# The four norm borders of a fused transformer kernel, row tile by row tile

## The chip, the cores and the metric

The kernel runs on one core of one Trainium2 chip. The metric is the device time of one execution in microseconds (us), lower is better. Each engine of the core (TensorE, VectorE, ScalarE, GpSimd, and SyncE, which only starts transfers here) runs its own list of instructions in the order in which the program wrote it, and waits for semaphores of the others. Nothing in such a list overtakes what stands ahead of it.

## The reference

The input x is 512 rows of 1024 numbers in float32. Three blocks and a feed-forward part follow each other, all of one form: normalise, project, mix, project back, normalise, add.

```python
def rms_norm(x, gain):
    y = xf * lax.rsqrt(jnp.mean(xf * xf, axis=-1, keepdims=True) + NORM_EPS)
    return y * gain
# hybrid_layer, twice (three kinds of attention between the projections)
h = rms_norm(x, g_pre);  p = h @ w_in
...
return x + rms_norm(y, g_post)
# second_block: a recurrence beside an attention, then a feed-forward part
h = rms_norm_2(x, pre_mix_norm[l]);  proj = h @ w_in[l]
...
x = x + rms_norm_2(mix, post_mix_norm[l])
h = rms_norm_2(x, pre_ffn_norm[l])
f = (jax.nn.silu(h @ w_ffn_gate[l]) * (h @ w_ffn_up[l])) @ w_ffn_down[l]
x = x + rms_norm_2(f, post_ffn_norm[l])
```

So there are four places at which x is normalised with a gain `g_pre` and then multiplied by weights: ahead of layer 0, of layer 1, of the third block and of the feed-forward part. They are called borders 0 to 3 here. At borders 1 to 3, and at the end of the kernel, the output y of the part before is first normalised with a gain `g_post` and added to x.

## The kernel before

**Tiles.** The 512 rows are four row tiles of 128. `x_res` holds x as [128, tile, 1024]. A product needs the normalised x the other way round, features on the partitions: `act_hl` holds it as eight chunks of 128 features by 512 rows. Every operand is split into a high part in a narrower format and a low part (what the high part leaves out), and each product of two numbers is three matmuls, high by high, high by low, low by high (`three`; lines 578 to 580 where the output's partitions are features, "feat", and 581 to 583 where they are rows, "tok").

**Weights.** They come as 274 blocks of 512 KB in a ring of four slots. SyncE loads a block into `w_raw` when the block four before it has been used; ScalarE makes its high part (`high`, line 792), GpSimd its low part (`low`, line 561), both into `w_hl`; then TensorE uses it in 24 matmuls of 512 columns. One dense group is four such blocks (BC = 2 chunks each) into banks 0 to 3.

**A border.** ScalarE and VectorE run `post(i)`: per row tile VectorE drains the last half of y from its bank (lines 1197, 1201), ScalarE squares it and makes the row's factor (`row_scale`, lines 799 to 803, 512 wide for y, since the other half was squared earlier in `first_half`, line 1018), VectorE multiplies y by the factor and by `g_post` (line 1467) and adds it to x (line 1469). ScalarE then squares x (line 799, 1024 wide) and VectorE multiplies the identity by the row's factor (line 1123, `diag`, which lies in `y_tok`). TensorE multiplies x by that diagonal: this transposes and scales at once (line 631, float32, which the chip does in two passes, 32 of them in a border, in two halves of four chunks). ScalarE takes the high part out of the bank with the gain as its scale (line 829), VectorE the low part (line 1135). The first four chunks are turned before the first weight block is used, the other four behind it. The first product needs all four row tiles.

**What sets the order.** `plan()` writes one list, STEPS, and each engine walks it, taking from each step what is its own. The last output projection before a border goes tile by tile (`tile_by_tile`), so that row tile 0 is done early. `high(b + 2)` is called at the first use of block b. At borders 1 and 2 ScalarE starts two more transfers on its own queue: `x_spill` (line 1075, x to memory, 2 MB) right behind the first high parts of the norm, and at border 2 with it `w_gates` (line 1077, 1 MB, the weights of the recurrence's gates), which TensorE wants at line 737.

**The end.** `post(3)` drains a tile of `y_ffn` one tile ahead of the arithmetic on it; each finished tile is stored by SyncE.

## Time and profile before

| | |
|---|---|
| median of 3 runs | 2050.96 us (2048.58 to 2052.0) |
| the profiled execution | 2051.6 us, of which its span 2049.8 us |
| TensorE matmul busy | 1941.4 us, 95% of the span, mean granted clock 0.966 |
| VectorE, ScalarE, GpSimd busy | 773.1, 886.3, 661.9 us |
| chain that ended last | TensorE 83%, VectorE 8%, ScalarE 5%, issue 3% |
| DMA | 163.80 MB, mean 80 GB/s |

Times in the profile count from the span's start. A row of the timeline gives the start and the duration of an instruction (or of several merged ones: x8), its engine, its line, what it writes and reads, and in brackets how long the engine sat idle before it and who ended that. The duration includes a fixed part that overlaps the next instruction: the distance between two starts is what an engine loses. In the stretches view, "PEclk" is the TensorE clock that was granted, as a share of full speed (1.0 is 2.4 GHz, 0.5 is 1.2 GHz). "128*128" in a matmul's row is the loaded operand.

### The profile page before, as it was taken

What the parts mean: (1) busy time and instruction counts of PE and PEld (TensorE: products, weight loads), DVE (VectorE), ACT (ScalarE), POOL (GpSimd) and SP (SyncE); (2) the same over time, 40 slices, a digit from 0 to 9 for tenths busy, and PEclk for the clock granted to TensorE, in tenths of its full rate; (3) what the DMA queues carried; (4) which work ended last, traced back from release to release, by engine and by line L of the source; (5) the groups of instructions that cost most, each with busy time, mean ns of one, the idle gap of its engine ahead of it and who ended that gap; (6) DMA issues with size and microseconds to landing.
All of it is one profiled execution on the core that took longest, in us unless ns stands there. A gap on an engine that the chain in (4) does not pass through costs nothing.

```text
span 2049.8 us, 25677 instructions
## 1 busy us (share of the span) xinstructions
PE 1941.4 (95%) x9552; PEld 1599.9 (78%) x9552; DVE 773.1 (38%) x1393; ACT 886.3 (43%) x1741; POOL 661.9 (32%) x278
## 2 busy tenths in 40 slices
PE   8998998998899899899889999999999989999998
PEld 6877787877777778787767788888788878888886
DVE  3434655344543555534444682111251431111102
ACT  4555564344455555444444652333453353322222
POOL 2422231321224132132123354434303424344442
PEclk9999999997899999999889999999999989999999
DMA  4221211211322112121032223222201322323222
GB/s 149 83 72 42 72 62 51 74 62 43 133 75 80 52 62 64 50 83 60 34 136 92 81 94 102 83 93 92 82 1 58 128 83 93 103 93 99 97 93 92
DMA packets 44572, 163.80 MB, mean 80 GB/s; under 512 B 6192, under 2 KB 6448, under 8 KB 43824
## 3 DMA queue, kind: packets, MB, share of 16 engines
q1 hardware_dynamic: 42640, 148.65, 21.9%
q10 hardware_dynamic: 1824, 13.63, 1.8%
q8 instruction: 77, 1.26, 0.2%
q14 instruction: 31, 0.25, 0.0%
HBM read 155.97 MB, written 6.29 MB: 79 GB/s over the span
## 4 chain that ended last, share of the span: by engine, by line
PE 83%; DVE 8%; ACT 5%; issue 3%; DMA 0%; POOL 0%; DVEq 0%; ACTq 0%; POOLq 0%; SPq 0%
PE bank L578 12%; PE bank L579 12%; PE bank L580 12%; PE bank L581 10%; PE bank L583 10%; PE bank L582 10%; PE bank L691 3%; PE bank L709 2%; PE bank L669 2%; PE bank L715 2%; PE bank L670 1%; ACT q_dup L904 1%; PE bank L711 1%; PE bank L667 1%; PE bank L631 1%
## 5 line engine op out<-in xcount | busy, mean ns | idle before, releaser
L561 POOL TENSOR_TENSOR w_hl<-w_raw,w_hl 128x1024 fp32r<-128x1024 f32 x274 | 661.7, 2420 | 1363.5 <-ACT w_hl L792 1362.8
L792 ACT ACTIVATE w_hl<-w_raw 128x1024 fp32r<-128x1024 f32 x274 | 287.4, 1058 | 344.8 <-DMA w_raw<-wstream 344.2
L578 PE MATMUL bank<-act_hl,w_hl 128*128 128x512 f32 x1056 | 428.2, 405 | 3.2 <-DVE act_hl L1135 2.5
L580 PE MATMUL bank<-act_hl,w_hl 128*128 128x512 f32 x1056 | 414.6, 393 | 0.0
L579 PE MATMUL bank<-act_hl,w_hl 128*128 128x512 f32 x1056 | 414.1, 392 | 0.0
L581 PE MATMUL bank<-w_hl,act_hl 128*128 128x512 f32 x672 | 265.7, 395 | 4.0 <-POOL w_hl L561 1.9
L583 PE MATMUL bank<-w_hl,act_hl 128*128 128x512 f32 x672 | 262.9, 391 | 0.0
L582 PE MATMUL bank<-w_hl,act_hl 128*128 128x512 f32 x672 | 262.7, 391 | 0.0
L578 PEld LDWEIGHTS bank<-act_hl,w_hl 128*128 128x128 f32 x1056 | 200.7, 190 | 45.6 <-DVE act_hl L1135 2.9
L580 PEld LDWEIGHTS bank<-act_hl,w_hl 128*128 128x128 f32 x1056 | 199.8, 189 | 43.7
L579 PEld LDWEIGHTS bank<-act_hl,w_hl 128*128 128x128 f32 x1056 | 200.6, 190 | 40.0 <-issue 1.9
L955 ACT ACTIVATE pt_hl<-bank 128x512 fp32r<-128x512 f32 (+3 forms) x128 | 56.0, 438 | 236.1 <-PE bank L691 235.7
L581 PEld LDWEIGHTS bank<-w_hl,act_hl 128*128 128x128 f32 x672 | 126.9, 189 | 31.8 <-issue 2.1
L583 PEld LDWEIGHTS bank<-w_hl,act_hl 128*128 128x128 f32 x672 | 126.9, 189 | 26.8
L582 PEld LDWEIGHTS bank<-w_hl,act_hl 128*128 128x128 f32 x672 | 127.1, 189 | 25.6
L1323 DVE TENSOR_TENSOR pt_hl<-bank,pt_hl 128x512 fp32r<-128x512 f32 (+3 forms) x128 | 62.5, 489 | 145.2 <-ACT pt_hl L955 144.5
L691 PE MATMUL bank<-ident,probs 128*128 128x128 f32 x508 | 94.4, 290 | 14.0 <-DVE pt_hl L1323 13.7
L1287 DVE TENSOR_REDUCE nmax<-bank 128x1 f32<-128x512 f32 (+3 forms) x128 | 60.2, 488 | 107.2 <-PE bank L678 105.9
L669 PE MATMUL bank<-k_hl,q_dup 128*128 128x512 f32 (+1 forms) x192 | 70.8, 369 | 16.6 <-DVE probs L1312 14.6
L1217 DVE TENSOR_TENSOR probs<-bank,probs 128x512 f32<-128x512 f32 x22 | 15.1, 688 | 186.4 <-PE bank L580 186.4
L581 PE MATMUL bank<-w_hl,y_hl 128*128 128x512 f32 x192 | 79.9, 416 | 5.2 <-DVE q_low L1231 5.2
L709 PE MATMUL bank<-vhl,pt_hl 128*128 128x128 f32 x320 | 84.6, 325 | 0.0
(216 smaller groups left out, 2907.9 us busy)
## 6 DMA issues: line engine op xcount, KB each, us to landing
w_raw<-wstream SPq DMA_DIRECT2D x274, 512.0 KB, 3.4
x_spill<-x_res ACTq DMA_DIRECT2D x2, 2048.0 KB, 6.9
x_res<-x_spill ACTq DMA_DIRECT2D x2, 2048.0 KB, 7.9
x_res<-x SPq DMA_DIRECT2D x4, 512.0 KB, 6.3
g_post<-post_gains ACTq DMA_DIRECT2D x4, 512.0 KB, 3.8
x_res<-x ACTq DMA_DIRECT2D x1, 2048.0 KB, 7.8
out<-x_res SPq DMA_DIRECT2D x4, 512.0 KB, 2.6
probs<-w_gates ACTq DMA_DIRECT2D x1, 1024.0 KB, 9.7
```

Source lines behind the costliest of these rows:

```text
L561: nc.gpsimd.tensor_tensor(w_hl[:, slot, 1].rearrange("p c n -> p (c n)"), w_raw[:, slot, :], w_hl[:, slot, 0].rearrange("p c n -> p (c n)" ...
L578: pe.matmul(out_ap, wh, ah, start=start, stop=False)
L579: pe.matmul(out_ap, wh, al, start=False, stop=False)
L580: return pe.matmul(out_ap, wl, ah, start=False, stop=stop)
L581: pe.matmul(out_ap, ah, wh, start=start, stop=False)
L582: pe.matmul(out_ap, ah, wl, start=False, stop=False)
L583: return pe.matmul(out_ap, al, wh, start=False, stop=stop)
L669: pe.matmul(to[:, 0:nb * P], q_dup[:, p, a, rows], k_hl[:, p, a, keys], start=True, stop=False)
L691: tr = pe.transpose(to[:, kb * P:(kb + 1) * P], probs[:, p_slot(kind, n, a), kb * P:(kb + 1) * P], ident[:, :])
L709: pe.matmul(o, pt_hl[:, slot, 0, keys], v.rearrange("p h d -> p (h d)"), start=(kb == 0), stop=False)
L792: nc.scalar.activation(w_hl[:, b % RING, 0].rearrange("p c n -> p (c n)"), w_raw[:, b % RING, :], ACT.Copy).then_inc(s_high_done, 1)
L1323: nc.vector.tensor_tensor(pt_hl[:, m % 3, 1, 0:nb * P], ps, pt_hl[:, m % 3, 0, 0:nb * P].bitcast(f32), ALU.subtract).then_inc(done, 1)
```

## The change

The four borders go row tile by row tile. `border(i, ...)` writes for each row tile t: drain and scale (`rows`), the turn of the tile (`normturn`), the sum of the next tile (`total`), and then those products of the first dense group whose rows are split. In "tok" groups (borders 0 and 1) that is a product per tile; in "feat" groups (borders 2 and 3) one per pair of tiles, in 256 columns. Blocks 0 and 1 of the group need chunks 0 to 3 of the norm, blocks 2 and 3 chunks 4 to 7.

The row factor and `g_pre` are now applied to rows, by one VectorE operation of 1024 columns into `y_acc` (`norm_row`), for which `g_pre` is a row repeated on 128 partitions (512 KB, as `g_post` was). TensorE transposes plainly, with the identity, eight transposes a tile into two banks. ScalarE's high part and VectorE's low part are two operations of 512 columns a tile. The sum y times factor times `g_post` plus x is three half-width operations instead of two full-width ones, and the first half of y has been multiplied by `g_post` ahead of the border (`half_gain`). The spill and the load of `w_gates` come behind the whole first group. The high parts of the group's blocks 4 and 5 are made when blocks 2 and 3 end. At the end of the kernel VectorE drains a tile and sums it, one after the other.

```diff
+    def border(i, dense_steps):
+        blocks, rest = dense_steps[:4], dense_steps[4:]
+        def part(ks, j):
+            if groups[blocks[0][2]]["orient"] == "tok":
+                return [blocks[k][:4] + ((j,),) for k in ks]
+            return [blocks[k] + (j,) for k in ks]
+        low, high = (0, 1), (2, 3)
+        if groups[blocks[0][2]]["orient"] == "tok":
+            after = [part(low, 0), part(low, 1) + part(high, 0), part(low, 2) + part(high, 1),
+                     part(low, 3) + part(high, 2) + part(high, 3)]
+        else:
+            after = [[], part(low, 0), part(high, 0), part(low, 1) + part(high, 1)]
+        out = [("rows", i, 0), ("total", i, 0)]
+        for t in range(TT):
+            out += [("rows", i, t + 1), ("normturn", i, t), ("total", i, t + 1)] + after[t]
+        return out + rest
...
     for l in range(DEPTH):
-        steps.append(("norm", l))
+        steps += border(l, project("qk", l, 0, 0))
         if l > 0:
             steps.append(("spill", l))
-        steps += project("qk", l, 0, 0)
         steps.append(("forget", l))
...
         steps += tile_by_tile(output(l, len(KINDS) - 1))
-        steps.append(("post", l))
-    steps.append(("norm", 2))
+    steps += border(2, dense("xr", DC, "feat", m=0))
     steps.append(("spill", 2))
-    steps += dense("xr", DC, "feat", m=0)
     lru = [("lru", part, c) for part in ("decide", "decay", "scale", "scan") for c in range(DC)]
...
-    steps.append(("norm", 3))
-    for m in range(FC // 2):
+    steps += border(3, dense("ffn", DC, "feat", m=0))
+    for m in range(1, FC // 2):
         steps += dense("ffn", DC, "feat", m=m)
     steps += dense("down", FC, "tok", m=0) + tile_by_tile(dense("down", FC, "tok", m=1))
-    steps.append(("post", 3))
+    for t in range(TT):
+        steps += [("rows", 4, t), ("total", 4, t)]
 
 
...
-        elif st[0] == "norm":
-            late.append(("normturn", st[1], 0))
-            pending = ("normturn", st[1], 1)
...
-            for c in NORM_CHUNKS[st[2]]:
-                take(("norm", st[1], c), 4 + c % 4)
+            for h in range(2):
+                take(("norm", st[1], st[2], h), 4 + 2 * (st[2] % 2) + h)
...
-    FIRST = [(ident, ident_in), (g_pre, gains)]
+    FIRST = [(ident, ident_in)]
...
-                if tiles[0] == 0 and (g["tag"], g.get("l", 0), g.get("ki", 0), g.get("m", 0)) in AFTER_NORM:
-                    for c in range(k * BC, (k + 1) * BC):
-                        pe.wait_ge(*drained(("norm", AFTER_NORM[g["tag"], g.get("l", 0), g.get("ki", 0), g.get("m", 0)], c)))
-                if tiles[0] == 0:
+                if (g["tag"], g.get("l", 0), g.get("ki", 0), g.get("m", 0)) in AFTER_NORM:
+                    i = AFTER_NORM[g["tag"], g.get("l", 0), g.get("ki", 0), g.get("m", 0)]
+                    for t in (tiles if half is None else (2 * half, 2 * half + 1)):
+                        pe.wait_ge(*drained(("norm", i, t, k // 2)))
+                if begins:
                     pe.wait_ge(s_low_done, b + 1)
+                cols = slice(0, S) if half is None else slice(half * S // 2, (half + 1) * S // 2)
...
+                        ws, as_ = (js, cols) if feat else (slice(None), js)
+                        mm = three(bank[j][:, cols], (w[:, 0, cc, ws], w[:, 1, cc, ws]),
...
+            def norm_turn(i, t):
+                pe.wait_ge(s_h_rows, i * TT + t + 1)
+                if i == 0 and t == 0:
+                    pe.wait_ge(s_first, 16 * len(FIRST))
+                for h in range(2):
+                    if earlier(("norm", i, t, h))[1] > 0:
+                        pe.wait_ge(*earlier(("norm", i, t, h)))
+                    to = bank_of(("norm", i, t, h))
+                    for c in range(4):
+                        at_ = (4 * h + c) * P
+                        tr = pe.transpose(to[:, c * P:(c + 1) * P], y_acc[:, t, at_:at_ + P], ident[:, :])
+                    tr.then_inc(filled(("norm", i, t, h)), 1)
...
+            def begin():
+                act.dma_start(g_pre[:, :], pre_gains[0:1, :].partition_broadcast(P)).then_inc(s_pre_gain_in, 16)
+                act.dma_start(g_post[:, :], post_gains[0:1, :].partition_broadcast(P)).then_inc(s_gain_in, 16)
+                act.preload_act_table_set("natural_log_exp_and_others")
+                act.wait_ge(s_setup, 1)
+            def norm_high(i, t):
+                for h in range(2):
+                    act.wait_ge(*full(("norm", i, t, h)))
+                    nc.scalar.activation(act_hl[:, 4 * h:4 * h + 4, 0, t * P:(t + 1) * P],
+                                         bank_of(("norm", i, t, h))[:, :].rearrange("p (c n) -> p c n", n=P), ACT.Copy)\
+                        .then_inc(s_norm_high, 1)
+            def rows(i, t):
+                if i == 0 or t == TT:
+                    return
+                if i > 2 and t == 0:
                     act.preload_act_table_set("natural_log_exp_and_others")
-                    act.wait_ge(s_setup, 1)
-                    for t in range(TT):
-                        norm_row(0, t)
-                    act.wait_ge(s_first, 16 * len(FIRST))
-
-                act.dma_start(g_post[:, :], post_gains[i:i + 1, :].partition_broadcast(P)).then_inc(s_gain_in, 16)
-                if i > 0:
-                    act.wait_ge(s_block_used, norm_blocks(i))
-
...
+                act.wait_ge(*drained(("dense", LAST[i - 1], t)))
+                row_scale(y_ffn if i == 4 else y_acc, t, 20, stat[:, 44 + t:45 + t]).then_inc(s_y_scale, 1)
+            def total(i, t):
+                if i == 4:
+                    return
+                if t < TT:
+                    norm_row(i, t)
+                elif i < 3:
+                    act.dma_start(g_pre[:, :], pre_gains[i + 1:i + 2, :].partition_broadcast(P)).then_inc(s_pre_gain_in, 16)
+                if t == TT and i > 0:
+                    act.dma_start(g_post[:, :], post_gains[i:i + 1, :].partition_broadcast(P)).then_inc(s_gain_in, 16)
...
-                    link(nc.scalar.activation(probs[:, 0, :], y[:, t, 0:D // 2], ACT.Square,
-                                              accum_out=stat[:, 40 + t:41 + t]))
+                    nc.scalar.activation(probs[:, t, :], y[:, t, 0:D // 2], ACT.Square,
+                                         accum_out=stat[:, 40 + t:41 + t]).then_inc(s_half_sq, 1)
+                act.wait_ge(s_half_sq, (i + 1) * TT)
...
+            begin()
             for st in STEPS:
                 if st[0] == "block":
-                    if st[4][0] == 0:
+                    begins, ends = st[4][0] == 0 and st[5:] != (1,), st[4][-1] == 3 and st[5:] != (0,)
+                    if ends if st[2] in BORDER and st[3] >= 2 else begins:
                         high(st[1] + 2)
...
+                elif st[0] == "rows":
+                    rows(*st[1:])
+                    if st[1:] == (0, 1):
+                        high(0)
+                elif st[0] == "total":
+                    total(*st[1:])
...
-                nc.vector.tensor_scalar(diag[:, t, :], ident[:, :], stat[:, 8 + t:9 + t], None, ALU.mult)\
-                    .then_inc(s_h_rows, 1)
-
...
+                nc.vector.scalar_tensor_tensor(out=y_acc[:, t, :], in0=x_res[:, t, :], scalar=stat[:, 8 + t:9 + t],
+                                               in1=g_pre[:, :], op0=ALU.mult, op1=ALU.mult).then_inc(s_h_rows, 1)
+            def norm_low(i, t):
+                for h in range(2):
+                    dve.wait_ge(s_norm_high, (i * TT + t) * 2 + h + 1)
+                    to = act_hl[:, 4 * h:4 * h + 4, :, t * P:(t + 1) * P]
+                    nc.vector.tensor_tensor(to[:, :, 1, :], bank_of(("norm", i, t, h))[:, :].rearrange("p (c n) -> p c n", n=P),
+                                            to[:, :, 0, :].bitcast(f32), ALU.subtract).then_inc(freed(("norm", i, t, h)), 1)
...
+            def rows(i, t):
+                if i > 0 and t < TT:
+                    drain(LAST[i - 1], range(t, t + 1))
+                if i < 4 and t > 0:
+                    norm_row(i, t - 1)
+            def half_gain(i):
                 y = y_ffn if i == 3 else y_acc
                 dve.wait_ge(s_gain_in, 16 * (i + 1))
                 for t in range(TT):
+                    dve.wait_ge(s_half_sq, i * TT + t + 1)
+                    ins = nc.vector.tensor_tensor(y[:, t, 0:COLS], y[:, t, 0:COLS], g_post[:, 0:COLS], ALU.mult)
+                link(ins)
+            def total(i, t):
+                if i > 0 and t < TT:
+                    y = (y_ffn if i == 4 else y_acc)[:, t, :]
+                    if t == 0 and i < 4:
+                        dve.wait_ge(s_x_back, 16 * i)
+                    dve.wait_ge(s_y_scale, (i - 1) * TT + t + 1)
+                    scale = stat[:, 28 + t:29 + t]
+                    link(nc.vector.scalar_tensor_tensor(out=y[:, COLS:D], in0=y[:, COLS:D], scalar=scale, in1=g_post[:, COLS:D],
+                                                        op0=ALU.mult, op1=ALU.mult))
+                    nc.vector.scalar_tensor_tensor(out=x_res[:, t, 0:COLS], in0=y[:, 0:COLS], scalar=scale,
+                                                   in1=x_res[:, t, 0:COLS], op0=ALU.mult, op1=ALU.add)
+                    nc.vector.tensor_tensor(x_res[:, t, COLS:D], x_res[:, t, COLS:D], y[:, COLS:D], ALU.add).then_inc(s_x_new, 1)
+                if i < 4 and t > 0:
+                    norm_low(i, t - 1)
+                if t == TT:
+                    if i == 0:
+                        setup_constants()
+                    if i < DEPTH:
+                        forget_weights(i)
```

TensorE at border 1, before: banks 4 to 7 take the turned chunks, bank 0 is row tile 0 of the first product (`w_hl` weights, `act_hl` normalised x).

```order
L631 MATMUL bank6<-y_tok_57,x_res_49 128x128
L631 MATMUL bank7<-y_tok_57,x_res_49 128x128
L581 MATMUL bank0<-w_hl_53,act_hl_51 128x512
L582 MATMUL bank0<-w_hl_53,act_hl_51 128x512
L583 MATMUL bank0<-w_hl_53,act_hl_51 128x512
```

The same place after (lines 589 to 591 are the product, line 644 is the transpose; bank 1 is row tile 1).

```order
L589 MATMUL bank0<-w_hl_53,act_hl_51 128x512
L590 MATMUL bank0<-w_hl_53,act_hl_51 128x512
L591 MATMUL bank0<-w_hl_53,act_hl_51 128x512
L644 MATMUL bank6<-ident_82,y_acc_60 128x128 x4
L644 MATMUL bank7<-ident_82,y_acc_60 128x128 x4
L589 MATMUL bank1<-w_hl_53,act_hl_51 128x512
```

Products of tile 0 now stand ahead of the transposes of tile 1, and each later turn stands behind the products of the tile before it.

ScalarE at border 2, before (`loaded2` is the arrival of a weight block in the ring's third slot, `bank_full6` of a turned chunk in its bank):

```order
L829 ACTIVATE act_hl<-bank,g_pre 128x512 [waits bank_full7]
L1075 DMA x_spill<-x_res 128x4096
L1077 DMA probs<-w_gates 128x2048
L792 ACTIVATE w_hl<-w_raw 128x1024 [waits loaded2]
L829 ACTIVATE act_hl<-bank,g_pre 128x512 [waits bank_full4]
```

The two transfers after (line 897 drains the first group's result, `block_used` is the end of its last block):

```order
L897 ACTIVATE xpad<-bank 128x512 [waits bank_full2]
L897 ACTIVATE xpad<-bank 128x512 [waits block_used]
L1092 DMA x_spill<-x_res 128x4096
L1094 DMA probs<-w_gates 128x2048
L801 ACTIVATE w_hl<-w_raw 128x1024 [waits loaded2]
```

Both transfers have moved from the middle of the norm to behind the last block of the first group.

VectorE at the end of the kernel, before:

```order
L1201 COPY y_ffn<-bank 128x512 [waits bank_full0,gain_in]
L1201 COPY y_ffn<-bank 128x512 [waits bank_full1]
L1467 SCALAR_TENSOR_TENSOR y_ffn<-y_ffn,stat,g_post 128x1024 [waits y_scale]
L1469 TENSOR_TENSOR x_res<-x_res,y_ffn 128x1024 [waits dve_step]
L1201 COPY y_ffn<-bank 128x512 [waits bank_full2]
```

And after (`y_scale` is ScalarE's row factor of the tile just drained):

```order
L1211 COPY y_ffn<-bank 128x512 [waits bank_full0,dve_step]
L1491 SCALAR_TENSOR_TENSOR y_ffn<-y_ffn,stat,g_post 128x512 [waits y_scale]
L1493 SCALAR_TENSOR_TENSOR x_res<-y_ffn,stat,x_res 128x512 [waits dve_step]
L1495 TENSOR_TENSOR x_res<-x_res,y_ffn 128x512
L1211 COPY y_ffn<-bank 128x512 [waits bank_full1]
```

The drain of a tile stood ahead of the sum of the tile before it; it now stands behind that sum.

## Rows read from the trace of the kernel before

**Rows 1.** The stretches view, three norm borders; columns: stretch, us, busy per engine, granted clock, DMA.
```profile
core 0: us, PE busy (x) PEld busy (x) DVE busy (x) ACT busy (x) POOL busy (x), PEclk, DMA share, GB/s
529.80:543.30 13.50, 7.74 (x33) 6.83 (x33) 10.15 (x14) 10.37 (x28) 0.00 (x0) 0.61 0.39 134
1057.60:1070.70 13.10, 6.77 (x32) 6.04 (x33) 9.74 (x14) 9.97 (x28) 0.00 (x0) 0.74 0.37 135
1662.10:1675.60 13.50, 7.35 (x34) 6.39 (x33) 10.15 (x14) 10.38 (x28) 0.00 (x0) 0.65 0.37 115
```

**Rows 2.** The timeline of TensorE; columns: start, duration, engine, line, operation, tiles, count, idle before.
```profile
543.28 0.76 PE L581 MATMUL bank<-w_hl,act_hl 128*128 128x512 f32 x1 [1.05 <-DVE act_hl L1135]
...
550.36 3.73 PE L631 MATMUL bank<-y_tok,x_res 128*128 128x128 f32 x32
...
570.26 0.40 PE L578 MATMUL bank<-act_hl,wff_hl 128*8 128x512 f32 x1
```

**Rows 3.** The timeline of ScalarE at the same border.
```profile
529.11 1.06 ACT L799 ACTIVATE probs<-x_res 128x1024 f32<-128x1024 f32 x1 [2.71 <-DVE x_res L1469]
...
530.73 0.61 ACT L799 ACTIVATE probs<-y_acc 128x512 f32<-128x512 f32 x1
...
531.80 0.20 ACT L803 ACTIVATE stat<-stat 128x1 f32<-128x1 f32 x1
...
541.05 1.84 ACT L829 ACTIVATE act_hl<-bank,g_pre 128x512 fp32r<-128x512 f32 x3 [1.27 <-PE bank L631]
```

**Rows 4.** The timeline of GpSimd just ahead of it.
```profile
521.96 4.78 POOL L561 TENSOR_TENSOR w_hl<-w_raw,w_hl 128x1024 fp32r<-128x1024 f32 x2 [7.78 <-ACT w_hl L792]
```

**Rows 5.** The timeline of VectorE in the same stretch.
```profile
525.00 2.82 DVE L1467 SCALAR_TENSOR_TENSOR y_acc<-y_acc,stat,g_post 128x1024 f32<-128x1024 f32 x1
...
529.00 0.69 DVE L1197 TENSOR_TENSOR y_acc<-bank,y_acc 128x512 f32<-128x512 f32 x1
529.60 1.28 DVE L1467 SCALAR_TENSOR_TENSOR y_acc<-y_acc,stat,g_post 128x1024 f32<-128x1024 f32 x1
```

**Rows 6.** The groups by line and form; columns after the bar: busy us, mean ns, idle before.
```profile
L1386 DVE SCALAR_TENSOR_TENSOR xc<-xpad,cw,xc 128x512 f32<-128x512 f32 x8 | 6.0, 752 | 0.3
```

**Rows 7.** The timeline of TensorE in layer 0: plain transposes, and matmuls of 512 and 256 columns.
```profile
54.86 1.91 PE L655 MATMUL bank<-ident,probs 128*128 128x128 f32 x16
...
109.83 0.39 PE L578 MATMUL bank<-act_hl,w_hl 128*128 128x512 f32 x1
...
110.51 0.28 PE L669 MATMUL bank<-k_hl,q_dup 128*128 128x256 f32 x1
110.62 0.28 PE L670 MATMUL bank<-k_hl,q_low 128*128 128x256 f32 x1
```

**Rows 8.** The stretches view, the first loads.
```profile
2.00:12.00 10.00, 3.95 (x17) 3.66 (x18) 0.86 (x3) 5.52 (x14) 0.00 (x0) 1.00 0.94 338
```

**Rows 9.** The timeline around the first border, ScalarE and TensorE.
```profile
13.18 1.06 ACT L792 ACTIVATE w_hl<-w_raw 128x1024 fp32r<-128x1024 f32 x1 [0.24 <-issue]
...
16.82 0.47 PE L581 MATMUL bank<-w_hl,act_hl 128*128 128x512 f32 x1 [1.90 <-POOL w_hl L561]
...
43.88 0.40 PE L578 MATMUL bank<-act_hl,wff_hl 128*8 128x512 f32 x1
```

**Rows 10.** The timeline at the third and fourth border: ScalarE's DMA queue, TensorE.
```profile
1069.70 0.45 ACTq L1077 DMA_DIRECT2D probs<-w_gates  x1
...
1096.18 0.39 PE L578 MATMUL bank<-act_hl,w_hl 128*128 128x512 f32 x1
...
1103.90 1.96 PE L737 MATMUL bank<-xc,probs 128*128 128x512 f32 x4 [2.12 <-issue]
...
1702.98 0.39 PE L578 MATMUL bank<-act_hl,w_hl 128*128 128x512 f32 x1
```

**Rows 11.** The page's DMA issues; columns: KB each, us from issue to landing.
```profile
probs<-w_gates ACTq DMA_DIRECT2D x1, 1024.0 KB, 9.7
```

**Rows 12.** The timeline of VectorE at the end of the kernel.
```profile
2032.38 0.69 DVE L1201 COPY y_ffn<-bank 128x512 f32<-128x512 f32 x1 [51.06 <-PE bank L583]
...
2045.50 1.22 DVE L1469 TENSOR_TENSOR x_res<-x_res,y_ffn 128x1024 f32<-128x1024 f32 x1
```

111 lines of the change are left out of this document (19 added, 92 removed).

## The prediction, made before the changed kernel ran

> **What bounds the kernel now.** I read the table first: TensorE is busy 95% of the span, and 83% of the chain that ended last is its own. So only stretches in which it has nothing to do count, and the change can win or lose just there. The stretches view of borders 1 to 3 [rows 1] shows them: from the last product of the part before to the first product behind the norm 13.5, 13.1 and 13.5 us pass, with VectorE and ScalarE busy some 10 us of each, GpSimd idle, and a granted clock of 0.61 to 0.74, a mix of the two levels. Then I read the timeline at border 1: the first product at 543.28, the second turn at 550.36, 3.7 us long, and the group's end at 570.26 [rows 2]. From there each engine's own timeline gives durations [rows 3 to 7].
>
> **Durations.** ScalarE: the factor of x keeps it 530.73 − 529.11 = 1.62 us, that of y 531.80 + 0.20 − 530.73 = 1.27, a high part of the norm (1.84 for three, merged) about 0.6 [rows 3]. GpSimd: a low part of weights 2.39 [rows 4]. VectorE: a drain 0.69, or 0.60 to the next start; 1024 columns 1.28; but the same line at 525.00 took 2.82, and ended at 527.82, 1.1 after GpSimd's operation did at 526.74 [rows 4, 5]. I read this as a lock: a VectorE operation with two inputs in SBUF waits until a running GpSimd one is through, while one that reads a bank (529.00) is not held. 512 columns with two SBUF inputs take 0.75 [rows 6]. TensorE: 16 plain transposes 1.91, so 0.11 each and 0.9 for a tile's eight; a 512-column matmul (110.51 − 109.83)/3 = 0.227, so 24 in a block 5.44 and a row tile of a block 1.36; a 256-column one 0.11 to 0.12 [rows 7].
>
> **Border 1, at full clock.** The sum of tile 0 can't begin before the lock opens at 526.74 [rows 4]. Then .78 + .69 + .61 for its three halves, 1.7 for x's factor with the handover, 1.3 for `norm_row`, 0.5 for four transposes, 1.3 for two high parts, and the first low part: the first product starts at about 534.9, 8.4 before 543.28 [rows 2]. Sixteen tile products take 21.8 and three more turns 2.7, together to 559.4. What TensorE waits for comes on top. Tile 1: its transposes are done at 538.5, but in VectorE's queue its low parts stand behind the sum of tile 2, and that sum behind y's factor of tile 2, which ScalarE takes only after the high parts of weight blocks 2 and 3. These start GpSimd twice, and the lock holds the sum 0.5 and 2.2 us. Tile 1's split is ready at 544.7: 6.2 us idle. Tiles 2 and 3: each turn stands behind 5.4 us of products, and bank, high part, low part take 1.3 while nothing else is queued: 2 × 1.3. The end is 559.4 + 6.2 + 2.6 = 568.2, or −2.1 against 570.26.
>
> The clock moves this. Before, the product at 543.28 shows 0.76 against 0.40 later [rows 2], and at the low level a tile product costs 1.2 more. TensorE is now idle twice, ahead of tile 0 and of tile 1, so I let two or three tile products run low: +3.0, end 571.2. The last loads (blocks 4 and 5 wait for slots that are freed later than before) may add 1. I take 0, range −2 to +2.
>
> **Border 2** the same way, in halves: the first product needs tiles 0 and 1 and starts at 1067.7, 3.0 before the edge of [rows 1]. Eight half blocks of 24 matmuls at 0.118 take 22.7 (0.9 more than four whole ones), two turns 1.8, and the wait ahead of the second half 1.4: 1093.6 against 1096.18 [rows 10], −2.6 at full clock, −0.7 with low stretches. I take −1.3, range −2.5 to 0.
>
> **Border 3.** Here no GpSimd operation holds the first sum. Laid out like border 2, the first product comes at 1672.4, 3.2 before the edge [rows 1], and the same 25.9 (22.7 + 1.8 + 1.4) leads to 1698.3, −4.7 against 1702.98 [rows 10]; with low stretches −3.1; with a late load −2. I take −3.5, range −4.7 to −2.
>
> **Border 0.** In the first 10 us the DMA engines are 94% busy at 338 GB/s [rows 8]. Two gain rows of 512 KB now go ahead of most of x and the first weights; they take 1.0 MB / 338 GB/s = 3.1 us of it (g_post went behind the weights before, so not all of that is new). ScalarE's queue holds the high part of weight block 0 ahead of tile 0's, and that of block 1 ahead of x's next factor, so a late weight holds the norm. Before, ScalarE took block 0 at 13.18 and products began at 16.82 [rows 9]. After, with loads 1.3 late, tile 1's products start at about 22.6; the 14 that are left take 19.1, two turns 1.8, two waits 2.6: 46.1 against 43.88 [rows 9]. With loads 2.6 late and low stretches 47.7, with loads in time 44.7. I take +2.7, range +0.8 to +4.
>
> **The gates' weights.** Before, `w_gates` was issued at 1069.70 [rows 10] and took 9.7 [rows 11], 26 us ahead of its use. After, it is issued about 1.1 behind the end of the first group (spill first, three drains before it), and lands 10.8 behind that end. TensorE took the gates 1103.90 − 1096.18 = 7.7 behind it [rows 10]. So at least 2.9 to 3.1 us of wait stand in its queue, with all later products behind them. The 3 MB now travel beside weight loads of 0.5 to 1 MB, which at [rows 8]'s rate is 1.5 to 3.1 more; part may be caught up. I take +4.5, range +2.9 to +7.
>
> **The tail.** VectorE's last sum ends at 2045.50 + 1.22 = 2046.72; its first drain starts at 2032.38 [rows 12]. Now a tile is one chain: drain .69, y's factor 1.3 [rows 3], halves .78 + .69 + .61, handovers .15, together 4.2, and the next drain behind it. Three of them and a last of 4.3 end at 2032.38 + 12.6 + 4.3 = 2049.3: +2.5, range +2.2 to +2.7. Nothing hides it, since TensorE is done before the last tile's turn comes. The extra `half_gain` operations lie beside products and cost nothing at borders 1 to 3; the lock on them is in the sum above only where it holds a first drain.
>
> **Sum.** +2.7 + 0 − 1.3 + 4.5 − 3.5 + 2.5 = +4.9 on the profiled 2051.6 would be 2056.5; on the median of 2050.96, which the new time will be compared with, 2055.9. I forecast 2055.9.
>
> **A rule against the change.** Plain transposes after layer 0 take 0.11 from one to the next while a row's own length is 0.27 to 0.29 [rows 7]. The Trainium skill, "TensorE: Matmul & The Clock Gate", section "Part 4: PE-mode transpose", gives about 275 ns for a transpose in a kernel and says of the clock gate that it "doesn't engage" for transposes. By the first, 32 transposes would add 32 × 0.165 = 5.3 us a border; the trace's spacing of 0.11 speaks against it here, since they are pipelined. By the second, the turns would count as idle; it is rival C below, and the trace of before can't show it.
>
> **Rivals.**
> A. Faster. The lock does not fall on the sums (GpSimd's low parts of blocks 2 and 3 land between them), and the gates' weights are hidden. At full clock border 1 then gives −5.8, border 2 −4.5, border 3 −4.8; with border 0 at +1.7 and the tail the sum is −10.9: 2040. For it: the two 2.4 us holds are most of the 6.2 idle at border 1. Against: both highs are made early, so something of VectorE's must meet them, and a landing of 9.7 can't fit in 7.7. It decides once the holds fall under 1 us and the gates' wait under 2.
> B. About the same. TensorE holds its full clock through all four borders: border 0 +2.3, then −2, −2.5, −4.7, +4.5, +2.5, sum +0.1: 2051. For it: work reaches TensorE earlier, and in pieces. Against: [rows 1] shows low clocks with idle stretches no longer than those of 6 to 7 us that I expect.
> C. Slower still. Short turns between waits leave the clock low over more of the borders: each border at its upper end (+4, +2, 0, −2) with the gates at +5 and the tail: +11.5, 2062. For it: the first 16 turns of before ran at 0.61. Against: after the first products the queue is never empty for more than 1.3 us.
>
> **Chances.** The forecast, 2053 to 2059, 0.50; A 0.12; B 0.26; C 0.12. What a measurement of this kernel can tell from no change is about 0.2%, 4.1 us: over 2055.1 is slower. Of the forecast's case some two thirds lie beyond that, of C all, of B little: slower 0.50, same 0.37, faster 0.13. The range, 2047 to 2061, leaves out most of A and half of C.
>
> **What would show it.** In the changed profile: the first product of border 1 near 535 to 536 and a gap of 5 to 7 us ahead of tile 1's products, with a half-width sum of 2.4 to 3 us beside a GpSimd row; gaps of about 1.3 behind later turns; the group's end 40 us behind the last product of layer 0; `w_gates` issued behind line 897's drains and a wait of 3 us or more ahead of the gates' first matmul; a spacing of 4.2 us between the last drains. I am wrong if TensorE's products start later than before at any border, if tile 1 waits less than 3 us, or if the gates don't wait.

## The result, and the profile after

The changed kernel takes 2059.94 us (median of 5 runs, 2059.77 to 2062.65) against 2048.84 for the kernel before (5 runs). The ratio is 1.0055, 95% interval 1.004 to 1.007: slower by some 11 us. A later series of 12 runs of the same kernel gave 2054.37 and a ratio of 1.0035 (1.0011 to 1.0058). Both ratios are above the 1.002 that the prediction took as the bound of what can be told, though the interval of the second begins below it. Both times lie in the range of the prediction, 2047 to 2061. Its centre, 2055.9, lies between them; the first is above the 2053 to 2059 that it called its own case. Two executions in the whole record ran at a far lower granted clock, one of the kernel before (2768.8 us at 0.65) and one of the kernel called best below (2195.3 us at 0.84), and the ratios leave them out.

The page of the changed kernel, busy time and chain:

```profile
PE 1926.5 (94%) x9616; PEld 1588.6 (77%) x9616; DVE 798.1 (39%) x1425; ACT 883.2 (43%) x1741; POOL 663.5 (32%) x278
...
PE 80%; DVE 8%; ACT 7%; issue 3%; DMA 1%; POOL 0%; DVEq 0%; SPq 0%; POOLq 0%; ACTq 0%
```

TensorE is busy 14.9 us less than before and the span is 8.4 us longer: it waits 23 us more, and that is where to look. Two spans are a poor measure of it, though, as the table shows. I divide each trace at the same places: the forget product behind border 0 and border 1, the last product ahead of each border, the end of the fourth weight block behind it, the first matmul of the gates, the end of the fifth block behind that one, the last product of all. Each number is the difference of two starts of the timeline.

| stretch, us | before, as shown | before, again | after, as shown | after, again |
|---|---|---|---|---|
| start to end of border 0 | 43.9 | 41.7 | 47.9 | 48.0 |
| layer 0 | 485.5 | 486.6 | 481.8 | 486.0 |
| border 1 | 40.9 | 39.3 | 39.3 | 39.1 |
| layer 1 | 486.6 | 486.4 | 489.0 | 482.8 |
| border 2 | 39.1 | 41.3 | 38.5 | 38.0 |
| to the first gates matmul | 8.0 | 8.0 | 12.1 | 12.1 |
| five blocks behind it | 37.0 | 38.7 | 39.7 | 39.4 |
| third block | 521.0 | 521.0 | 521.4 | 521.4 |
| border 3 | 40.9 | 40.5 | 38.2 | 38.1 |
| feed-forward part | 337.3 | 337.3 | 338.4 | 338.5 |
| tail | 9.7 | 9.7 | 11.9 | 11.9 |
| span | 2049.8 | 2050.4 | 2058.2 | 2055.0 |

Without the two layers, in which TensorE has the same instructions in all four traces, the stretches sum to 1077.6 and 1077.4 before, and to 1087.4 and 1086.3 after. The change costs 9 to 10 us where it acts. The layers add or take some us that differ between executions of the same kernel: together 972.1 and 973.0 before, 970.8 and 968.8 after. The stretches view of the layers shows what differs (changed kernel, layers 0 and 1; columns as in [rows 1]):

```profile
47.89:529.71 481.82, 450.31 (x2368) 370.92 (x2367) 231.11 (x464) 241.52 (x535) 136.99 (x58) 0.97 0.20 66
569.04:1058.02 488.98, 458.28 (x2369) 377.35 (x2367) 231.21 (x464) 242.02 (x535) 137.03 (x58) 0.95 0.21 69
```

The same again, kernel before:

```profile
43.88:529.41 485.53, 455.81 (x2369) 376.11 (x2367) 229.30 (x460) 240.38 (x535) 133.95 (x56) 0.95 0.20 65
```

TensorE's work is the same, 2368 or 2369 matmuls (VectorE has four more operations after the change, `half_gain`); the granted clock is 0.97 in the short stretch and 0.95 in the long ones. That is 31 us at the low level in the short one, 48 and 51 in the long ones, and most of the difference lies in the last 60 us of the layer, its last attention: 14 against 31.

**Border 1.** TensorE's timeline in the changed kernel, answering [rows 2]:

```profile
532.09 1.09 PE L644 MATMUL bank<-ident,y_acc 128*128 128x128 f32 x8 [1.99 <-DVE y_acc L1140]
534.75 0.80 PE L589 MATMUL bank<-w_hl,act_hl 128*128 128x512 f32 x1 [1.56 <-DVE act_hl L1147]
...
540.03 1.43 PE L644 MATMUL bank<-ident,y_acc 128*128 128x128 f32 x8
543.96 0.57 PE L589 MATMUL bank<-w_hl,act_hl 128*128 128x512 f32 x1 [2.50 <-DVE act_hl L1147]
...
551.14 1.03 PE L644 MATMUL bank<-ident,y_acc 128*128 128x128 f32 x8
553.15 0.50 PE L589 MATMUL bank<-w_hl,act_hl 128*128 128x512 f32 x1 [0.97 <-DVE act_hl L1147]
...
569.04 0.40 PE L586 MATMUL bank<-act_hl,wff_hl 128*8 128x512 f32 x1
```

The first product comes at 534.75 (predicted 534.9), the end at 569.04. Tile 1 is waited for 2.50, and 2.90 in the second trace. The turns of tiles 2 and 3 are each followed by a gap of 0.97: bank, high part, low part, with nothing else queued. GpSimd and VectorE at the wait ahead of tile 1, answering [rows 4] and [rows 5]:

```profile
536.86 5.29 POOL L569 TENSOR_TENSOR w_hl<-w_raw,w_hl 128x1024 fp32r<-128x1024 f32 x2 [9.89 <-ACT w_hl L801]
```

```profile
538.94 1.01 DVE L1491 SCALAR_TENSOR_TENSOR y_acc<-y_acc,stat,g_post 128x512 f32<-128x512 f32 x1 [1.78 <-ACT stat L812]
539.98 2.72 DVE L1493 SCALAR_TENSOR_TENSOR x_res<-y_acc,stat,x_res 128x512 f32<-128x512 f32 x1
542.62 0.68 DVE L1495 TENSOR_TENSOR x_res<-x_res,y_acc 128x512 f32<-128x512 f32 x1
543.23 1.27 DVE L1147 TENSOR_TENSOR act_hl<-bank,act_hl 128x512 fp32r<-128x512 f32 x2
```

The two holds are there: 1.01 and 2.72 instead of 0.75, and the split of tile 1 (its low parts) begins at 543.23. That an operation which reads a bank is not held is shown by the kernel before, whose GpSimd row in [rows 4] runs from 521.96 to 526.74:

```profile
524.39 0.69 DVE L1197 TENSOR_TENSOR y_acc<-bank,y_acc 128x512 f32<-128x512 f32 x1 [1.86 <-PE bank L583]
```

**Border 0**, ScalarE's first weight block and TensorE, answering [rows 9]:

```profile
13.77 1.06 ACT L801 ACTIVATE w_hl<-w_raw 128x1024 fp32r<-128x1024 f32 x1 [6.13 <-DMA w_raw<-wstream]
```

```profile
17.40 0.77 PE L589 MATMUL bank<-w_hl,act_hl 128*128 128x512 f32 x1 [6.32 <-POOL w_hl L569]
...
20.10 0.63 PE L589 MATMUL bank<-w_hl,act_hl 128*128 128x512 f32 x1
...
21.38 0.63 PE L589 MATMUL bank<-w_hl,act_hl 128*128 128x512 f32 x1
...
24.38 0.50 PE L589 MATMUL bank<-w_hl,act_hl 128*128 128x512 f32 x1 [0.98 <-DVE act_hl L1147]
31.99 0.50 PE L589 MATMUL bank<-w_hl,act_hl 128*128 128x512 f32 x1 [0.98 <-DVE act_hl L1147]
39.59 0.50 PE L589 MATMUL bank<-w_hl,act_hl 128*128 128x512 f32 x1 [0.98 <-DVE act_hl L1147]
...
47.89 0.40 PE L586 MATMUL bank<-act_hl,wff_hl 128*8 128x512 f32 x1
```

Three matmuls lie between 20.10 and 21.38, so 0.43 each instead of 0.227: TensorE runs at the low level until about 22. Tile 0's twelve matmuls take 4.97 to the start of the next turn at 22.37, 2.2 more than at full clock. Then come three gaps of 0.98.

**The gates and the tail.** The first gates matmul, the issues ahead of it on ScalarE's queue, and the page's row, answering [rows 10, 11]; then VectorE's last tile, answering [rows 12]:

```profile
1096.86 0.33 ACTq L1092 DMA_DIRECT2D x_spill<-x_res  x1
...
1097.23 0.45 ACTq L1094 DMA_DIRECT2D probs<-w_gates  x1
...
1108.65 3.78 PE L746 MATMUL bank<-xc,probs 128*128 128x512 f32 x4 [6.37 <-DMA probs<-w_gates]
```

```profile
probs<-w_gates ACTq DMA_DIRECT2D x1, 1024.0 KB, 11.4
```

```profile
2038.64 0.69 DVE L1211 COPY y_ffn<-bank 128x512 f32<-128x512 f32 x1 [48.66 <-PE bank L591]
...
2042.74 0.68 DVE L1211 COPY y_ffn<-bank 128x512 f32<-128x512 f32 x1
...
2054.42 0.68 DVE L1495 TENSOR_TENSOR x_res<-x_res,y_ffn 128x512 f32<-128x512 f32 x1
```

`w_gates` lands 11.4 after its issue, TensorE waits 6.4 for it, and its four matmuls then take 3.78 where they took 1.96: the low level again. The drains of the tail are 4.10 apart.

### The profile page after: what moved, and what is told of

Read it like the earlier page. It is cut to its first block, busy times and chain, and to the rows that moved or that the text cites. A ratio compares the mean times of both kernels' runs of the same rounds, so it can differ in the third digit from the quotient of the medians.

```text
span 2058.2 us, 25844 instructions
## 1 busy us (share of the span) xinstructions
PE 1926.5 (94%) x9616; PEld 1588.6 (77%) x9616; DVE 798.1 (39%) x1425; ACT 883.2 (43%) x1741; POOL 663.5 (32%) x278
## 4 chain that ended last, share of the span: by engine, by line
PE 80%; DVE 8%; ACT 7%; issue 3%; DMA 1%; POOL 0%; DVEq 0%; SPq 0%; POOLq 0%; ACTq 0%
PE bank L586 12%; PE bank L588 12%; PE bank L587 12%; PE bank L589 10%; PE bank L591 10%; PE bank L590 10%; PE bank L700 3%; PE bank L718 2%; PE bank L678 2%; PE bank L724 2%; PE bank L679 1%; ACT q_dup L928 1%; PE bank L676 1%; PE bank L720 1%; DVE y_tok L1271 1%
## 5 line engine op out<-in xcount | busy, mean ns | idle before, releaser
L586 PE MATMUL bank<-act_hl,w_hl 128*128 128x512 f32 (+1 forms) x1120 | 442.7, 395 | 5.5 <-issue 3.9
L588 PE MATMUL bank<-act_hl,w_hl 128*128 128x512 f32 (+1 forms) x1120 | 428.5, 383 | 0.0
L587 PE MATMUL bank<-act_hl,w_hl 128*128 128x512 f32 (+1 forms) x1120 | 428.0, 382 | 0.0
L586 PEld LDWEIGHTS bank<-act_hl,w_hl 128*128 128x128 f32 x1120 | 215.7, 193 | 46.7 <-issue 8.4
L588 PEld LDWEIGHTS bank<-act_hl,w_hl 128*128 128x128 f32 x1120 | 214.6, 192 | 41.3
L587 PEld LDWEIGHTS bank<-act_hl,w_hl 128*128 128x128 f32 x1120 | 215.6, 192 | 38.3 <-issue 2.2
L966 ACT ACTIVATE probs<-bank,nmax 128x256 f32<-128x256 f32 (+3 forms) x144 | 73.3, 516 | 22.4 <-DVE nmax L1297 21.0
```

The lines of the kernel that those rows point to most:

```text
L586: pe.matmul(out_ap, wh, ah, start=start, stop=False)
L587: pe.matmul(out_ap, wh, al, start=False, stop=False)
L588: return pe.matmul(out_ap, wl, ah, start=False, stop=stop)
L966: nc.scalar.activation(ps if in_bank else row, ps, ACT.Exp, bias=nmax[:, par, b:b + 1], accum_out=sums[:, par, a:a + 1])\
```

## Experiments

Twelve runs, two of them the two kernels again. They were made in three series on three chips; each ratio is to the kernel before, run in the same series on the same chip. What decides are the stretches, each read from one trace of a run.

**The kernel before, again.** 

> The kernel before, unchanged, once more with a profile. What it tells apart: the changed kernel's trace shows TensorE's clock low for 13.6 us at the end of layer 0's last attention, the shown trace of before for 30.8 us, and there the later start of 4.0 us from the first border disappears. Theory A (the low stretch in the shown trace of before was an accident of that execution): this trace shows less than 20 us low between 470 and 512, its span is 2046 to 2048, and the difference to the changed kernel's span is 10 to 12. Theory B (it belongs to the kernel before): again about 30 us low there and a span near 2049.8.

Ratio 0.9998 (0.9989 to 1.0007), span 2050.4. Layer 0 took 486.6, with 30.7 us of low clock between 470 and 512. Theory B holds for this trace. But the long low stretch does not belong to the kernel before: b_gates below, which is the same kernel up to border 2, shows a layer 0 of 482.3 us with 17 us of it. Of the 28 layers in the 14 traces, 15 have 31 us of low clock in their last 60 us and 13 have 14 to 17. In the three traces of the kernel before and b_gates it is 5 of 6 layers, in the others 10 of 22; whether the change moves these odds is not shown.

**The changed kernel, again.** 

> The changed kernel, unchanged, once more. In a_gain0, twelve runs fell into a group at 2051 to 2054 and one at 2057 to 2060, and the traces so far show the two attention stretches of a layer at 482 to 483 us with 31 to 34 us of low clock in them, or at 485 to 489 with 44 to 51. Theory (the five runs of the changed kernel, all at 2059.8 or above, were all drawn from its slower group; its stages alone are worse by 9 to 10 us): more runs show both groups, 2052 to 2054 and 2060, and the ratio to before falls from 1.0055 to 1.003 to 1.005. Rival (the changed kernel always has the long low stretches, and its 11 us are all its own): every run above 2058.

Ten of 12 runs lie at 2053.4 to 2056.8, one at 2062.7, and one at 2080.2. Neither theory's wording fits fully: the runs at 2060 are a minority and there is a lower group, as the first said, and the ratio fell to 1.0035. By the stretches 1 to 2 of the 11 us first measured were the draw, by the ratio of this series about 4.

**Transfers at border 2.** Three kernels. First, both issued behind the fourth turn:

```diff
+            if (i, t) == (2, TT - 1):
+                out.append(("spill", 2))
+            out += after[t]
...
-    steps.append(("spill", 2))
```

> The changed kernel with one thing undone: at border 2 the spill of x and the load of w_gates are issued right behind the fourth turn and its gain loads, ahead of the last products, instead of behind the whole first group. My theory: the gates' wait of 6.4 us ahead of the first gates matmul falls back to about 2.1, and the low clock behind it (2.7 us) goes too, so 7.0 us less than the changed kernel, about 2053. Rival: the wait is for the convolution on VectorE, which started later: then it stays above 5 us and the time stays near 2060. Second rival: the 3 MB now collide with the weight loads of the same group and give 2 to 3 us back at border 2's end: 2055 to 2056.

Ratio 1.0029 (1.002 to 1.0038), yet the stretch from layer 1's last product to the fifth block behind the gates took 90.0 us, as in the changed kernel (90.4). The total is smaller since both layers took 482.7. TensorE in this kernel:

```profile
1079.03 0.36 PE L588 MATMUL bank<-act_hl,w_hl 128*128 128x256 f32 x1 [1.02 <-issue]
...
1097.31 0.77 PE L588 MATMUL bank<-act_hl,w_hl 128*128 128x512 f32 x1 [6.53 <-ACT xpad L899]
...
1105.55 1.96 PE L748 MATMUL bank<-xc,probs 128*128 128x512 f32 x4 [0.94 <-issue]
```

The gates' own wait is gone, but an equal one stands ahead of weight block 4. ScalarE shows its real cause:

```profile
1092.46 1.06 ACT L803 ACTIVATE w_hl<-w_raw 128x1024 fp32r<-128x1024 f32 x1 [13.77 <-DMA w_raw<-wstream]
```

Block 4's load was issued at 1082.3, when 4 MB were under way (the two gains, spill, `w_gates`; the last of them now took 15.9), and landed 10.1 later. My theory for this place fell; the second rival's collision is there, and costs all of the 6 us and not 2 to 3. That the time, 2055.2, lies where this rival put it is luck of the layers. The next kernel has the condition `(i, t) == (2, TT - 2)`, behind the factor of x's last tile:

> The changed kernel, with the spill and the load of w_gates issued at border 2 right behind the factor of x's last row tile, five us earlier than in a_gates, where 4 MB met the loads of weight blocks 4 and 5 (they came at 1092.5 and 1095.6, and TensorE waited 6.5 us for them). The stretch from layer 1's last product to the end of the fifth weight block behind the first gates matmul took 84.0 and 87.9 us in two executions of the kernel before, 90.4 in the changed kernel, 90.0 in a_gates. My theory now (the two transfers need a place where no weight block is awaited; then nothing of this stretch is slower): 82.5 to 85. Rival (each place costs the same, since 3 MB must pass beside weights): 88 or more. The other stretches as in the changed kernel; total 2051 to 2055, with the drift of the clock in the attentions on top.

Ratio 1.0025 (1.0014 to 1.0037); the stretch took 86.3: 38.0, 9.7 to the gates, 38.6. `w_gates` took 9.5, block 4 was waited for 1.3. That is between my bound of 85 and the rival's 88: four of the six us come back. The two traces of the kernel before took 84.0 and 87.9 here, so what is left is within what they differ by. Against the shorter one it is 1.8 more ahead of the gates, 1.3 of them the wait for block 4, whose load took 6.1 instead of 3.4, and 1.6 more behind the gates' first matmul, with 3.4 us at the low level. Last, the reverse, in the kernel before:

```diff
     steps.append(("norm", 2))
+    steps += dense("xr", DC, "feat", m=0)
     steps.append(("spill", 2))
-    steps += dense("xr", DC, "feat", m=0)
```

> The kernel before with this one part of the change done: spill and w_gates are issued behind the whole first group of the third block. The same stretch from layer 1's last product to the fifth block behind the first gates matmul: my theory, about 84 to 88 plus the 6.5 that the late landing cost in the changed kernel (4.2 of wait and 2.3 of low clock behind it): 91 to 94, and the whole 5 to 7 us slower than before. Rival (the wait comes from the new border's order, not from the transfers): below 88, and no slower than before.

Ratio 1.003 (1.0021 to 1.004), 6 us; the stretch took 92.3. TensorE:

```profile
1102.09 3.78 PE L737 MATMUL bank<-xc,probs 128*128 128x512 f32 x4 [6.38 <-DMA probs<-w_gates]
```

The same wait and the same slow matmuls as in the changed kernel, without any of its other parts. Ahead of the gates it takes 12.2 instead of 8.0, and the five blocks behind them 39.5 instead of 37.0 and 38.7. This part of the change costs 5 to 7 us by itself.

**The tail.**

```diff
-    for t in range(TT):
-        steps += [("rows", 4, t), ("total", 4, t)]
+    steps.append(("rows", 4, 0))
+    for t in range(TT):
+        steps += ([("rows", 4, t + 1)] if t + 1 < TT else []) + [("total", 4, t)]
```

> The changed kernel with the tail's order undone: VectorE drains a tile of the last product one tile ahead of the sum, the three half-width operations stay. My theory: the 2.2 us of the tail come back, and since three halves take 2.08 to the next drain where the two full-width operations took 2.45, one more us: 2056.5 to 2058 (2.2 to 3.5 less than the changed kernel). Rival: the tail is bound by TensorE's last tile and the stores, and nothing changes: 2060.

The tail took 8.3 instead of 11.9, 3.6 less, and 1.4 less than before the change: with the old order the three halves are a gain. The median of 2050.81 (ratio 1.0012, 1.0001 to 1.0022) flatters it, since the layers took 482.7 each.

**Border 0.** g_post of layer 0 loaded behind the border:

```diff
-                act.dma_start(g_post[:, :], post_gains[0:1, :].partition_broadcast(P)).then_inc(s_gain_in, 16)
...
-                if t == TT and i > 0:
+                if t == TT:
                     act.dma_start(g_post[:, :], post_gains[i:i + 1, :].partition_broadcast(P)).then_inc(s_gain_in, 16)
```

> The changed kernel with g_post of layer 0 loaded behind the first border instead of at the start (512 KB less ahead of x and the first weights). Theory DMA (the first border is late because loads are late): weight blocks arrive 1.5 us earlier and the border's end moves from 47.9 to 46.4, total 1.5 less, about 2058.4. Theory order (ScalarE's queue and the idle time behind each turn make it late): the first weights arrive earlier but the border's end moves less than 0.7 us, total 2059.5 or more.

Border 0 took 45.1 instead of 47.9, ratio 1.0031 (1.0019 to 1.0044). ScalarE's first weight block came at 11.82 instead of 13.77, the first product at 15.46 instead of 17.40. Theory DMA holds: the loads are 1.9 us earlier where it said 1.5. The other 0.8 is the clock's: tile 0's twelve matmuls took 4.16 instead of 4.97, as the low level ended sooner behind their start. The 12 runs fell in two groups, 2051.4 to 2053.8 and 2057.1 to 2060.3. Then all repairs together, and with the four factors of x ahead of the first weight block:

```diff
                 act.wait_ge(s_setup, 1)
+                for t in range(TT):
+                    norm_row(0, t)
...
                 if t < TT:
-                    norm_row(i, t)
+                    if i > 0:
+                        norm_row(i, t)
```

> The changed kernel with four repairs: transfers as in a_gates2, the tail's drains one tile ahead, g_post of layer 0 loaded behind the first border, and all four factors of x ahead of the first weight block on ScalarE at border 0. By stages against the changed kernel: border 0 from 47.9 to 43.5 (a_gain0 gave 45.1), transfers -6, tail -3.6. Sum -14 against 2059.9: about 2046, so 3 to 5 us faster than before. Rival (border 0 is bound by the low parts of weights on GpSimd and by the idle time behind each turn, not by ScalarE's order): border 0 stays above 44.8, the total above 2047.

Ratio 1.0007 (0.9995 to 1.0019). Border 0 took 47.3, 2.2 more than in a_gain0: the rival's number holds, and border 0 is not bound by ScalarE's order as I had it. The reordering put the first product 0.9 later. The other 1.3 lie in tile 0's twelve matmuls: the second weight block's low part made TensorE wait once more (16.39, then 19.71), about 0.6, and the rest is low clock.

```profile
16.39 0.77 PE L592 MATMUL bank<-w_hl,act_hl 128*128 128x512 f32 x1 [4.91 <-POOL w_hl L572]
...
19.71 0.76 PE L592 MATMUL bank<-w_hl,act_hl 128*128 128x512 f32 x1 [0.42 <-POOL w_hl L572]
```

**Turns one product step earlier in TensorE's queue.**

```diff
+            held = after[t - 1][-1:] if t > 1 else []
+            out += [("rows", i, t + 1), ("normturn", i, t)] + held + [("total", i, t + 1)]
...
+            out += after[t] if t in (0, TT - 1) else after[t][:-1]
```

> all4, and the turns of row tiles 2 and 3 stand one product step earlier in TensorE's queue, so that bank, high part and low part of a turn (0.98 us of idle time at each in the changed kernel) lie beside that product. Theory (these gaps are pure queue order): about 1 us less at each of the turns that have a gap: border 0 -2, border 1 -2, borders 2 and 3 -1 each, so 5 to 6 under all4, near 2041. Rival (the turn then waits for norm_row on VectorE, and the gap moves ahead of the turn): gaps of the same sum stand ahead of line 644's rows, and less than 2 us are won.

Ratio 0.9982 (0.997 to 0.9995). Against all4: border 0 −2.6, border 1 −0.9 (with 3.4 us more of low clock), border 2 −0.7, border 3 −1.5, together 5.7. The gaps of about 1 us behind the turns of tiles 2 and 3 are gone, and none stands ahead of those turns: the theory holds. Then without the x factors' reordering:

> all4_pipe without the one repair that made things worse: at border 0 ScalarE's first weight block stands again ahead of the factors of x's tiles 1 to 3. Border 0 was 45.1 in a_gain0 and 47.3 in all4, which differ in that order; all4_pipe took 2.6 from all4 there. Theory: border 0 at 42.5 to 43, 2 less than in all4_pipe, all other stages as there; against the kernel before by stages: border 0 +0 (41.7 and 43.9 there), border 1 -2, border 2 with the gates -2, border 3 -4, feed-forward part +1.2, tail -1.4, so 7 to 9 us less, ratio 0.9960. Rival (the difference at border 0 was the clock's): border 0 at 44 to 45, ratio 0.998.

2042.95 us, ratio 0.9961 (0.9947 to 0.9976): 8 us faster than the kernel before by the ratio, and 11 faster than the changed kernel in the same series. Without the two layers its stretches sum to 1068.0, 9 to 10 less than before the change and 18 to 19 less than after it. Border 0 took 44.1, not the 42.5 I expected. Here the rival held: all twelve matmuls of tile 0 ran at the low level, longer than in a_gain0 (second tile at 23.09 against 21.63). Against all4_pipe, which differs only in the order, border 0 is 0.6 shorter; the 2.2 between a_gain0 and all4 were the order's only in part. The borders:

```profile
526.55:563.09 36.54, 30.06 (x130) 24.08 (x129) 20.55 (x27) 16.89 (x40) 6.53 (x3) 0.86 0.28 87
1045.37:1081.93 36.56, 29.62 (x225) 28.63 (x224) 19.29 (x23) 17.88 (x41) 6.47 (x3) 0.86 0.52 184
1649.38:1685.96 36.58, 29.73 (x225) 28.74 (x224) 19.29 (x23) 18.12 (x41) 7.98 (x4) 0.86 0.24 84
```

They take 36.6 each, against 39 to 41 before the change. Eleven of its 12 runs again fell in two groups, six at 2034.5 to 2040.1 and five at 2045.8 to 2047.3; the trace is of the fastest.

**Matmuls in place of plain transposes.**

```diff
-                        tr = pe.transpose(to[:, c * P:(c + 1) * P], y_acc[:, t, at_:at_ + P], ident[:, :])
+                        tr = pe.matmul(to[:, c * P:(c + 1) * P], y_acc[:, t, at_:at_ + P], ident[:, :], start=True, stop=True)
```

> The changed kernel with each plain transpose of line 644 written as a float32 matmul with the identity (same data, two passes, as the kernel before turned). 
Ratio 1.0068 (1.0052 to 1.0084). The borders in the changed kernel, and in this one:

```profile
529.71:569.04 39.33, 31.33 (x131) 24.73 (x129) 20.55 (x27) 16.47 (x40) 6.98 (x3) 0.87 0.23 81
1058.02:1096.54 38.52, 30.56 (x226) 29.36 (x224) 19.79 (x23) 18.18 (x42) 8.35 (x4) 0.87 0.26 94
```

```profile
531.68:573.78 42.10, 33.80 (x163) 27.53 (x161) 20.81 (x27) 16.14 (x39) 5.26 (x2) 0.92 0.23 76
1059.61:1098.49 38.88, 32.70 (x257) 31.94 (x256) 20.00 (x23) 18.43 (x42) 8.36 (x4) 0.96 0.28 91
```

The granted clock of the borders rises from 0.87 to 0.92 and 0.96, that is from 10.2 us at the low level to 6.8 and 3.4; border 3, not shown, has 3.4 too. The 6.8 of border 1 says little, since a_gain0 shows it there with plain transposes; at borders 2 and 3 every trace with plain transposes and early halves has 10.2, but for 6.8 at border 3 of all4_pipe. Borders 1 to 3 became longer by 2.8, 0.4 and 0.8, and only the first of them by the 2.5 to 3 of theory Pipeline. So part of the 11 did come back, as the rival said. The Trainium skill, "TensorE: Matmul & The Clock Gate", section "Part 4: PE-mode transpose", says that a transpose "doesn't count as PE-busy the same way". The fall from 10.2 to 3.4 agrees with it in direction. But a turn now also keeps TensorE busy for 2.05 instead of 1.09, and this run doesn't separate the two.

**Borders 2 and 3 in whole blocks** (`after = [[], [], [], blocks]` for "feat"):

> The changed kernel with borders 2 and 3 in whole blocks: their products of 512 columns begin when all four row tiles are split, as before the change, and the turns of all four come first. What it tells: what early halves are worth. Theory (the halves hide 12 us of products beside VectorE's rounds): the first product comes at 4 rounds of VectorE, some 12 us later than in the changed kernel, four blocks take 21.8 instead of 23.4 and the turns and gaps 3.7 less: borders 2 and 3 are each 5 to 7 us longer, but the wait for the next weight block (0 to 1.3) goes. Rival (VectorE's rounds are free once GpSimd is quiet, so little is lost): each 0 to 2 us longer.

Ratio 1.0105 (1.0085 to 1.0126). At border 2 the first product comes 21.6 behind layer 1's last one, 11.3 later than in the changed kernel. Border 2 took 45.0, border 3 44.4, against 38.0 to 38.5 and 38.1: 6.3 to 7 longer, as the theory had it. The wait of 1.2 ahead of the next block is gone (feed-forward part 337.3).

## Why the prediction was right in its range and low in its sum

The time and the sign fell where they were put, and most steps show in the traces. But the stretches add up to +9.7 and +8.9 where the sum had +4.9, and two of its three signs of being wrong came: TensorE's products start later than before at border 0 (17.40 and 17.35 against 16.82 and 16.23), and tile 1 at border 1 waits 2.50 and 2.90 us, less than 3. The gates do wait. By terms (after minus before, first the pair of traces as shown, then the pair run again):

- **Border 0: +2.7 predicted, +4.0 and +6.3 measured.** This is the term that was most mis-sized. From tile 1's first product to the end it took 23.5, as the sum had it (19.1 + 1.8 + 2.6); tile 1's first product came at 24.38 instead of 22.6, so the miss lies ahead of it. What the sum lacked is the clock: TensorE had done eight transposes and nothing else until 17.40, and tile 0's twelve matmuls cost 2.2 more than at full clock. The kernel before had 3.4 us at the low level there in one trace and none in the other, which with its earlier start is why the two differences lie 2.3 apart. The loads are the other part, and a_gain0 sizes it: without the second gain's 512 KB they come 1.9 earlier.
- **Border 1: 0, and −1.5 and −0.2.** The holds by GpSimd's operations came nearly as written, 0.3 and 2.0 more than 0.75 (predicted 0.5 and 2.2). The row at 529.00, cited for operations that are not held, stands behind GpSimd's and can't show it; the one at 524.39 does. The first product came within 0.15 us, partly by luck: the terms listed for it add up to 534.3 with 0.65 for a low part, and not to 534.9. The gap ahead of tile 1 was 2.5, not 6.2: the twelve matmuls ahead of it ran at the low level and took 5.3 instead of 2.7, and its low parts came 0.7 sooner. So here the low clock cost nothing, since it filled a wait; the +3.0 that I added for it counted some of this time twice.
- **Border 2: −1.3, and −0.6 and −3.3**; **border 3: −3.5, and −2.7 and −2.4**, and 1.2 of these are given back in the feed-forward part as a wait for the next weight block, the late load that was the lower end of that term. With it the term is −1.6 and −1.2.
- **The gates: +4.5 predicted, in the range +2.9 to +7.** Measured +4.2 of wait, as the landing sum had it, and 0.7 to 2.7 of low clock behind it, which it did not have. b_gates shows the whole, 5 to 7, by itself. The mechanism was right: beside weight loads the 1 MB landed after 11.4 instead of 9.7, 1.7 more where I had 1.5 to 3.1.
- **The tail: +2.5, and +2.1 and +2.2**, at the lower end of its range of +2.2 to +2.7 or just under it. Steps of 4.10 instead of 4.2.
- **Transposes.** A turn of eight takes 1.03 to 1.09 at full clock, 0.11 apart, as the rows of before had it, and not eight times 0.275.

Rival A is excluded: the holds are there, and the gates waited. Rival B needed full clock at all borders; the changed kernel's were at 0.87. Rival C's mechanism, low clock over the borders, was no worse at borders 1 to 3 than in the sum, but it was the case at border 0 and behind the gates' wait: the truth lies between the forecast and C. What had no place in the prediction at all is that the two layers, in which TensorE's work is untouched, move by 4 us and more each between executions.

What stays open: why the low stretches in the attentions are long in one execution and short in the next, and how much of border 0's loss is the low clock's own. No kernel here was made to tell. Nor was it tried to take GpSimd's holds away, so that they cause the gap ahead of tile 1 is read from the order and the rows, not from an experiment.

## What to carry to other kernels

Finer steps start a consumer earlier, but each small step then stands in a queue behind the last one's products: put the next producer one step ahead in that queue, and the gaps go (5.7 us here). When a change moves a border, list the transfers it carries along and ask what weight load each will meet: the same 3 MB cost nothing amid the norm, some 2 to 3 us behind the factor of the last row tile, and 5 to 7 behind the fourth turn or behind the group. Where identical stretches differ between executions by as much as the effect, compare stretch by stretch, not total by total.

## What had not been expected of the hardware

The same 2368 matmuls of a layer took 481.8 to 489.0 us in 14 traces, with 31 to 51 us of low clock in them. Most of what differs lies in the last attention, which has 14 to 17 us of it or 31. The runs of a kernel fell in groups whose means are 7 to 9 us apart (in the best one 2034.5 to 2040.1 and 2045.8 to 2047.3). That the two come from the same thing is likely and not shown. A short wait costs twice: TensorE's four gates matmuls behind 6.4 us of idling took 3.78 instead of 1.96, and the five blocks behind it 0.7 to 2.7 more. A load of one 512 KB block beside 4 MB of others landed only after 10.1 us (a_gates), against a median of 3.4.
